# Moving the rounding of a weight block, its remainder and the release of its buffer ahead of the key norm in the differential projections

## The reference, cut to what matters

```python
xn = rms_norm(h, ln_attn_pre)
proj = xn @ w_in                                # [512, 1024] @ [1024, 1792 + 1536]
# RWKV part: r, k, v and three low-rank inputs; then, per head of 64:
decay = exp(-DECAY_SCALE * sigmoid(w_decay0 + tanh(w_lo) @ w_decay_up))
a = sigmoid(w_iclr0 + a_lo @ w_iclr_up)
kk = k * k_k
kk = kk / maximum(norm(kk), 1e-12)              # the key norm
k = k * (1 + (a - 1) * k_a)
# differential part:
dq, dk, dv = split(proj[..., 1792:], 3)         # 512 columns each
```

## Time and profile before

| what | value |
|---|---|
| time, median of 3 executions | 2084.48 us (2080.75 to 2088.95) |
| the profiled execution's own time | 2084.6 us |
| its span in the profile | 2082.8 us |
| TensorE busy | 1995.6 us, 96% of the span |
| VectorE busy | 1020.9 us, 49% |
| ScalarE busy | 761.6 us, 37% |
| GpSimd busy | 217.5 us, 10% |
| mean granted TensorE clock | 0.982 of full speed |

### The profile page before, as it was taken

How to read it: one execution, slowest core, us unless ns; L and a number is a source line. 1 busy time by engine, 2 the same in 40 slices (tenths; PEclk the granted TensorE clock), 3 DMA queues, 4 the chain that set the end, 5 groups by cost and what they waited for, 6 DMA issues and landing times.

```text
span 2082.8 us, 25115 instructions
## 1 busy us (share of the span) xinstructions
PE 1995.6 (96%) x9824; PEld 1635.4 (79%) x9824; DVE 1020.9 (49%) x1363; ACT 761.6 (37%) x1142; POOL 217.5 (10%) x262
## 2 busy tenths in 40 slices
PE   7999899999999999999999999989889979999997
PEld 6876688888888777788888887868789758888885
DVE  5445444334336746343344337576643466656424
ACT  3235442222225465442222225253543444333322
POOL 4000010000002202010000004012732120000000
PEclk9999899999999999999999999999999999999998
DMA  6310023322222201122332223320101213332221
GB/s 182 100 41 6 21 81 101 101 88 93 102 101 66 74 14 48 41 91 94 101 100 81 101 101 92 101 61 21 38 5 42 81 43 98 101 101 81 101 101 40
DMA packets 140699, 158.08 MB, mean 76 GB/s; under 512 B 15944, under 2 KB 129616, under 8 KB 140624
## 3 DMA queue, kind: packets, MB, share of 16 engines
q1 hardware_dynamic: 139328, 155.01, 23.3%
q0 software_dynamic: 1296, 2.05, 0.4%
HBM read 153.36 MB, written 3.68 MB: 75 GB/s over the span
## 4 chain that ended last, share of the span: by engine, by line
PE 85%; DVE 9%; ACT 3%; issue 2%; DMA 0%; SPq 0%; POOL 0%; ACTq 0%; DVEq 0%; POOLq 0%
PE bank L2602 33%; PE bank L2622 15%; PE bank L2253 14%; PE bank L2278 2%; PE bank L2363 2%; PE bank L2333 2%; PE bank L2641 2%; PE bank L2349 1%; PE bank L2581 1%; DVE XL L1472 1%; PE bank L2443 1%; ACT w_hi L966 1%; PE bank L2306 1%; DVE w_lo L1465 1%; PE bank L2406 1%
## 5 line engine op out<-in xcount | busy, mean ns | idle before, releaser
L2602 PE MATMUL bank<-XH,w_hi 128*128 128x512 f32 x1008 | 398.5, 395 | 0.8 <-DVE w_lo L1749 0.8
L2602 PE MATMUL bank<-XH,w_lo 128*128 128x512 f32 x1008 | 393.4, 390 | 0.0
L2602 PE MATMUL bank<-XL,w_hi 128*128 128x512 f32 x1008 | 393.2, 390 | 0.0
L2602 PEld LDWEIGHTS bank<-XH,w_hi 128*128 128x128 f32 x1008 | 189.3, 188 | 42.1 <-DVE w_lo L1749 1.6
L2602 PEld LDWEIGHTS bank<-XH,w_lo 128*128 128x128 f32 x1008 | 189.2, 188 | 40.1
L2602 PEld LDWEIGHTS bank<-XL,w_hi 128*128 128x128 f32 x1008 | 189.4, 188 | 38.7 <-issue 0.5
L2253 PE MATMUL bank<-XH,w_hi 128*128 128x512 f32 x504 | 202.2, 401 | 4.1 <-DVE w_lo L1465 2.1
L2253 PE MATMUL bank<-XL,w_hi 128*128 128x512 f32 x504 | 197.6, 392 | 0.0
L2253 PE MATMUL bank<-XH,w_lo 128*128 128x512 f32 x504 | 197.5, 392 | 0.0
L2622 PE MATMUL bank<-XL,w_hi 128*128 128x512 f32 x480 | 186.8, 389 | 0.0
L2622 PE MATMUL bank<-XH,w_hi 128*128 128x512 f32 x480 | 186.7, 389 | 0.0
(11 more groups left out here) (402 smaller groups left out, 3370.8 us busy)
## 6 DMA issues: line engine op xcount, KB each, us to landing
w_raw<-in_ffn_w_gate SPq DMA_DIRECT2D x22, 1024.0 KB, 5.3
w_raw<-in_ffn_w_up SPq DMA_DIRECT2D x22, 1024.0 KB, 5.3
w_raw<-in_ffn_w_down SPq DMA_DIRECT2D x22, 1024.0 KB, 4.9
w_raw<-in_w_up SPq DMA_DIRECT2D x22, 1024.0 KB, 5.0
w_raw<-in_w_in SPq DMA_DIRECT2D x13, 1024.0 KB, 5.3
w_raw<-in_w_down SPq DMA_DIRECT2D x11, 1024.0 KB, 4.9
w_raw<-in_even_w_in SPq DMA_DIRECT2D x9, 1024.0 KB, 5.2
w_raw<-in_even_w_out SPq DMA_DIRECT2D x4, 1024.0 KB, 5.1
```

Of the source, the lines that this page charges most:

```text
L2602: m = pe.matmul(bank[b][:, :], w[:, k, P * c:P * (c + 1)], x[:, k, :], start=(k == 0 and j == 0), stop=(k == KT - 1 and j == 2))
```

## The change

The order within three engines' programs changes; no computation is added or removed.

- VectorE: `key_norm(t)` comes ahead of `query_key(2 * t + 1)`. The remainder of the next weights comes, for t = 1 to 3, directly behind `decays(t)`, ahead of both; for t = 0 it comes behind them, as before, but the norm is now ahead of the tile.
- ScalarE: the rounding of the same weights comes, for t = 1 to 3, behind the scaled copy, ahead of the three exponentials; for t = 0 behind the exponentials and ahead of the root.
- TensorE: in units 0 to 3 `tick(u)` comes ahead of `key_sums(j)`, no longer behind it.

```diff
@@ ScalarE, for t in range(4): @@
                     act.activation(RT[:, 3, :], aa[:, t, :], ACT.Identity, scale=V("k_a_2", t),
                                    bias=ka1[:, t:t + 1])
+                    if t >= 1:
+                        split(diff[t + 1] + 1)
                     act.wait_ge(rw_d, t + 1)
                     act.activation(RT[:, 2, :], RT[:, 4, :], ACT.Exp, scale=DS)
                     act.activation(RT[:, 4, :], RT[:, 4, :], ACT.Exp, scale=-DS)
                     act.activation(RT[:, 0, :], RT[:, 0, :], ACT.Exp, scale=-DS).then_inc(rw_exp, 1)
+                    if t == 0:
+                        split(diff[t + 1] + 1)
                     act.wait_ge(rw_max, t + 1)
                     link(act.activation(RT[:, 1, :], RT[:, 1, :], ACT.Ln, scale=2.0 ** 30))
                     act.activation(RT[:, 1, :], RT[:, 1, :], ACT.Exp, scale=-0.5, bias=epsb[:, 2:3]).then_inc(rw_rn, 1)
-                    split(diff[t + 1] + 1)
@@ VectorE @@
                 for t in range(4):
                     decays(t)
+                    if t >= 1:
+                        split(diff[t + 1] + 1)
+                    key_norm(t)
                     query_key(2 * t + 1)
-                    key_norm(t)
+                    if t == 0:
+                        split(diff[t + 1] + 1)
                     if t == 3:
                         dve.wait_ge(rw_pre, 8)
                         dve.memset(ABD, 0.0).then_inc(abd_zero, 1)
-                    split(diff[t + 1] + 1)
                     keys_of(t)
@@ TensorE, units j of diff_in @@
                             if t == 1:
+                                tick(u)
                                 key_sums(j)
...
-                    tick(u)
+                    if j >= 4:
+                        tick(u)
```

## The result

The changed kernel takes 2073.27 us (median of 8 executions, 2068.72 to 2078.46), the kernel before 2084.13 us (8 executions, 2080.75 to 2090.03). The ratio is 0.995 with a 95% interval of 0.9936 to 0.9965: 7 to 13 us less. The forecast was 2073.8 us.

What follows compares the result with a forecast made beforehand. Groups, not TensorE's units, were taken to set the stage's pace. Gains of 2.3 + 3.2 + 3.2 + 2.3 = 11.0 us, limited by TensorE to 10.8, gave 2084.6 - 10.8 = 2073.8 us; range 2069 to 2080 us.

Steps and rivals of the forecast that it cites:

- What bounds: In the stage, the group sets the pace: 16.8 us between `keys_of` starts, against 11 us of products and 1 us of sums.
- Groups 1 and 2: The rounding is hidden and VectorE runs without a hole: 3.2 us gained in each of the two groups.
- So the root is covered by the tile: Groups 1 and 2: the root takes 2.15 us from the norm's start, while norm and tile last 2.1 us.
- Group 0 and group 3: `keys_of(0)` starts at 1375.9, not 1378.24, 2.3 us gained; in group 3 the remainder's wait goes, 2.18 + 0.16 = 2.3 us.
- What is late next: At the values' fourth mean TensorE is later than VectorE by 0.3 us, so the stage ends 10.8 us earlier.
- The clock: TensorE's clock stays up over 1.5 us of idleness ahead of group 3's sums, which gives back 1.7 us.
- the rival's price: Clock-down rival: the 1.5 us gap ahead of group 3's sums halves the clock, 1.7 us come back, 2075.5 us; chance 0.2.
- The port: GpSimd's first product becomes ready under VectorE's remainder: GpSimd waits, VectorE loses nothing; if shared, up to 1.29 us per group.
- No effect at the end: Rival: the time comes back in the attention, the recurrence or an overlooked wait, about 2083 us; chance 0.14.
- More: Rival: a clock episode behind the stage also goes, 13 us gained, 2071; chance 0.05.

Runs made afterwards that it cites:

- The wider gap: The changed kernel with about 1.2 us of repeated memsets on VectorE in group 2, ahead of the norm; stage 95.57 us.
- the repetition: The changed kernel run again, five rounds, with no edit; 2073.41 us, ratio to before 0.9951, stage 92.88 us.
- the norm uncovered: The changed kernel with `key_norm` behind `query_key` again in groups 1 to 3; stage 95.85 us, +3.0.

## Why the prediction was right

On the clock of the trace before (0.91 us is added to the times after, since that stage began 0.91 us sooner):

| step | forecast | measured |
|---|---|---|
| `keys_of(0)` starts | 1375.9 | 1375.83 |
| time to spare behind the rounding, group 1 | 0.6 us | 0.5 to 0.6 us |
| `keys_of(1)` starts | 1389.5 | 1389.55 |
| `keys_of(2)` starts | 1403.0 | 1403.29 |
| sums of group 3 start | 1408.7 | 1408.96 |
| `keys_of(3)` starts | 1417.4 | 1417.88 |
| fourth mean starts | 1423.8 | 1424.15 |
| stage shorter by | 10.8 us | 10.5 us |
| time | 2073.8 us | 2073.27 us (median) |

**What bounds.** That groups and not units set the pace was right: 10.5 us came out of a stage in which TensorE's and VectorE's work stayed the same. The new order of root, rounding and remainder makes 10.0 us of it without the tick; the tick alone makes nothing (103.24 us) and is worth 0.4 us beside that order. One reading was too broad: "TensorE computes units 1 to 3 ... with the clock at full speed" holds for units 1 and 2. Ahead of the sums of group 2 TensorE had stood idle longest, and the clock fell there as well:

```profile
1400.64 1.85 PE L2836 MATMUL bank<-arena,con 128*128 128x512 f32 x2 [4.58 <-ACT arena L1316]
```

```profile
1400.60:1404.20 3.60, 3.56 (x7) 2.18 (x8) 3.44 (x7) 0.73 (x2) 0.00 (x0) 0.54 0.02 5
```

It changes nothing in the sum: unit 3 was still done 2.92 us before its sums could start, so this slow stretch cost the stage no time.

**Groups 1 and 2.** The term "3.2 us" for each was too large: 16.79 - 13.72 = 3.07 us for group 1, and 16.71 - 13.74 = 2.97 us for group 2. The step that was mis-sized is "So the root is covered by the tile". From the start of the norm `keys_of` takes 2.21 us to begin (1386.43 to 1388.64), not 2.15 (whose own parts, 0.72 + 1.30 + 0.1, make 2.12), and the norm and the tile cover 1.98 us, not 2.1. That leaves the hole of 0.23 us in both groups. (The "4.3 us" of a tile and `decays` is 4.4 by its parts; measured are 4.3 us from the end of the last product of `keys_of(0)`, 1379.78, to the remainder's start, 1384.11.)

**Group 0 and group 3.** 2.3 us and 2.3 us were forecast. Group 0 gave 2.4 us. Group 3 gave 16.73 - 14.59 = 2.1 us: the forecast counted the 0.16 us ahead of the clearing of `ABD` as gained, and it stayed. All four groups gave 10.6 us and not 11.0, and so `keys_of(3)` was late (1417.88 against 1417.4), which is behind most of the 0.3 us by which the stage missed.

**What is late next.** Right in kind: VectorE and TensorE met at the fourth mean. Forecast was that TensorE would be the later by 0.3 us; measured is VectorE, by 0.2 us (15.19 against 15.0 us behind the sums). TensorE needed 0.1 us less than counted (15.0 against 15.1 us), and VectorE's first subtraction came 0.5 us later (1422.50 + 0.91 = 1423.4 for its start, which the forecast put at 1422.9).

**The clock.** The forecast took 1.5 us of idleness as harmless; it was 1.67 us, and harmless. This was a choice between rows, not something that I could work out: the gap came out a hundredth of a us below the 1.68 us of the earlier trace rows, which the clock did not survive, so that this term came true is partly luck. It is not the luck of one execution, though. In the stage's eleven traces all 14 idle stretches of 0.72 to 1.67 us ahead of the sums left the clock at 1.00, and all eight of 2.23 to 4.66 us brought it down. The wider gap shows the rival's price to be real, 1.6 us.

**The port.** GpSimd paid and VectorE did not, as the order of the two said. The rule named beside that (the Trainium skill, SBUF — State Buffer, "SBUF: two separate sides") has whoever starts first hold the pair for the whole instruction, and the traces agree: 1.57 us for a product that needs 1.29, beside a remainder of 2.28 us. The product ended 1.16 us behind the remainder's end, and with the tick put back, where it began earlier under the remainder and took 1.84 us, 1.15 us behind it. The forecast's "near 1.9 us" for this product was too long: it became ready only 0.4 us before the remainder's end.

**No effect at the end** is excluded by the totals' interval: the medians fell by 10.9 us and, in the repetition, by 10.2. "More" cannot be told: the first profile's further 3.4 us lie within what identical code varies. That the median agrees to 0.5 us is partly luck. Its own interval is 3 us to either side; the stage says 10.5, which from the median before, 2084.13 us, would be 2073.7.

Not tried: what the sums of squares would gain from a second buffer for `RT[:, 1, :]`, so that a group's square need not wait for the last product of the group before.

## What to carry to other kernels

In a kernel whose matrix engine is busy 96% of the span, look for the stage in which it is not, and there read which queue has nothing left to do: reordering independent work on one engine (a root and a rounding) was worth 3.0 to 3.1 us in each of two groups, while releasing the buffer earlier was worth nothing until that was done. Each instruction that another engine will wait for should have cover behind it on the waiting engine; count that cover to a tenth, for it is what decides. And measure such a change between two events of its own stage (here to 0.03 us) and not by the total, which varies by 10 us between executions of the same kernel.

## What the runs showed of the hardware

- The clock after idleness of TensorE. In this stage 1.43 us and 1.67 us of idleness left the granted clock at 1.00; 2.23 us brought it to 0.67 over the next 4 us, 2.92 us to 0.57 and 3.13 us to 0.58. In the first block's attention 1.68 us were enough, so the length of the gap alone does not decide.
- The 4 us at a clock of 0.58 cost 1.6 us where TensorE is the bound. Where it waits for VectorE afterwards such a stretch cost nothing, as in group 2 of the kernel before and in group 2 with the norm uncovered.
- Small instructions wait too: with GpSimd's products behind `keys_of`, a copy of 128x8 on VectorE, 0.17 us alone, took 1.07 us beside a GpSimd product that had begun first. In group 3 of the same kernel the running sum took 2.33 us and not 1.23, beside a product that began 0.03 us before it.
